# A Hyena long convolution: two of its three index exchanges go by DMA through DRAM instead of TensorE transposes, and the turn is ordered in phases

## The reference

```
hy = dwconv1d(hy_in, p['hy_conv_w'], p['hy_conv_b'])
v, x1, x2 = split(hy, 3)                         # 512 channels each, 2048 latent + 128 context tokens
k_f = hyena_filter_fft(L, ...)                   # rfft, length 2L, of an MLP's taps times a decay
z = x1 * fft_long_conv(v, k_f[:, 0], bias[0])
z = x2 * fft_long_conv(z, k_f[:, 1], bias[1])    # the second order needs the first one's z
# fft_long_conv(u, k_f, b) = irfft(rfft(u, n=2L) * k_f)[:L] + u * b
```

## Time and profile before

| | |
|---|---|
| median of 3 runs | 3146.26 us (3144.06 to 3146.97) |
| profiled execution, own time | 3143.5 us |
| its span | 3141.7 us |
| mean granted TensorE clock | 0.97 of full speed |
| busy, share of span | TensorE 94%, weight loads 81%, DVE 54%, ACT 30%, POOL 21% |
| `hyena` within the span | about 639 us to 1265 us |
| DMA | 252.84 MB, 80 GB/s over the span |

### The profile page before, as it was taken

The page is one execution under the profiler, slowest core; times in us unless marked ns, Lnnn a source line. Parts: engine busy times, 40 slices in busy tenths (PEclk is TensorE's granted clock), DMA queues, the critical chain, the costliest instruction groups (busy, mean ns, idle before and its releaser), DMA issues. The chain is left out here.

```text
span 3141.7 us, 40466 instructions
## 1 busy us (share of the span) xinstructions
PE 2947.5 (94%) x16404; PEld 2547.7 (81%) x16404; DVE 1689.8 (54%) x1888; ACT 928.5 (30%) x1608; POOL 668.8 (21%) x344
## 2 busy tenths in 40 slices
PE   5999999979999998598899999999999999999998
PEld 3777887878888888577788888888888887788886
DVE  6664564556666666464575565565565563322223
ACT  5443434145545554355510100100100103211111
POOL 3133233102222221344132222222222210000000
PEclk7999999989999999799999999999999999999999
DMA  6111221422121211444411111111111105322222
GB/s 228 69 58 70 73 79 63 123 118 86 56 86 61 82 59 53 135 134 154 154 35 55 48 34 55 48 34 55 48 34 55 48 25 190 119 75 75 82 86 72
DMA packets 92739, 252.84 MB, mean 80 GB/s; under 512 B 14846, under 2 KB 53246, under 8 KB 83198
## 3 DMA queue, kind: packets, MB, share of 16 engines
q1 hardware_dynamic: 92608, 251.00, 23.5%
HBM read 175.01 MB, written 75.96 MB: 80 GB/s over the span
## 5 line engine op out<-in xcount | busy, mean ns | idle before, releaser
L1813 PE MATMUL out_up_banks<-xh_rest,up_w_hi 128*128 128x512 f32 (+2 forms) x1408 | 493.6, 351 | 9.4 <-DVE xl_rest L1923 7.3
L1813 PE MATMUL out_up_banks<-xh_rest,up_w_lo 128*128 128x512 f32 (+2 forms) x1408 | 493.7, 351 | 0.0
L1813 PE MATMUL out_up_banks<-xl_rest,up_w_hi 128*128 128x512 f32 (+2 forms) x1408 | 493.4, 350 | 0.0
L1969 DVE SCALAR_TENSOR_TENSOR ffn_hidden<-grid,params,ffn_hidden 128x2048 f32<-128x2048 f32 x176 | 457.7, 2601 | 24.6 <-DVE ffn_hidden L1966 0.2
L2125 PE MATMUL down_banks<-down_hi,down_h_hi 128*128 128x512 f32 x748 | 293.4, 392 | 11.3 <-DVE down_gate L2206 5.3
L1813 PEld LDWEIGHTS out_up_banks<-xh_rest,up_w_hi 128*128 128x128 f32 x1408 | 266.5, 189 | 40.9 <-DVE xl_rest L1923 8.1
L2125 PE MATMUL down_banks<-down_lo,down_h_hi 128*128 128x512 f32 x748 | 292.6, 391 | 0.0
L2125 PE MATMUL down_banks<-down_hi,down_h_lo 128*128 128x512 f32 x748 | 292.5, 391 | 0.0
L1813 PEld LDWEIGHTS out_up_banks<-xl_rest,up_w_hi 128*128 128x128 f32 x1408 | 266.3, 189 | 30.7
L136 POOL TENSOR_TENSOR up_w_hi<-up_w_whole,zero 128x1024 fp32r<-128x1024 f32 x44 | 124.2, 2822 | 779.9 <-PE out_up_banks L1813 763.3
L1813 PEld LDWEIGHTS out_up_banks<-xh_rest,up_w_lo 128*128 128x128 f32 x1408 | 266.3, 189 | 28.3
(11 more groups left out here) (267 smaller groups left out, 5773.3 us busy)
## 6 DMA issues: line engine op xcount, KB each, us to landing
hidden_ff_dram<-ffn_hidden SPq DMA_DIRECT2D x22, 1088.0 KB, 4.8
up_w_whole<-w_up_in SPq DMA_DIRECT2D x44, 512.0 KB, 5.2
pre_dram<-in_result SPq DMA_DIRECT2D x16, 1088.0 KB, 4.0
down_h<-hidden_ff_dram SPq DMA_DIRECT2D x88, 192.0 KB, 2.3
wada_late<-w_ada_late_in SPq DMA_DIRECT2D x32, 512.0 KB, 3.7
down_x<-w_down_in SPq DMA_DIRECT2D x22, 512.0 KB, 3.7
in_w_whole<-w_in_in SPq DMA_DIRECT2D x20, 512.0 KB, 4.5
home<-x_rows_in SPq DMA_DIRECT2D x17, 512.0 KB, 6.7
```

The source lines that it names most:

```text
L1813: last = pe.matmul(out, weight[:, u, k], in_block(value, rest, b, k), start=(k == 0 and j == 0), stop=(k == KM - 1 and j == 2))
L1969: last = nc.vector.scalar_tensor_tensor(out=y, in0=window, scalar=weight, in1=y, op0=ALU.mult, op1=ALU.add)
```

## The change

The forward exchange of the convolution and the exchange of the filter leave TensorE. `first` becomes a single matmul per batch (table as weights, rows as 512 moving columns), whose result lies with frequency and slot in the partitions and channels in the free dimension. ACT copies it to one of four buffers `sent`; SP writes the 256 KB of a batch to a scratch tensor in DRAM and, once this has landed, reads them back in another order into `spectrum` (16 partitions of 32 pieces of 512 bytes). The read of batch j-2 stands in SP's queue behind the write of batch j. The filter does the same by `f_sent` and `f_spectrum`. The 64 transposes of `turn_back` and `f_turn_back` per turn and their 16 DVE copies are gone; `turn_pairs`, the back exchange, stays on TensorE.

The turn is ordered in phases: head (`turn_rows`, `first`), then a stretch of `taps`/`f_first` while the data are exchanged, then `second`/`back1`, then `turn_pairs`/`back2` with `f_second`. Gates and the stored z are moved at the turn's start, decay or v ahead of the back half, and ACT issues the modulation loads. `taps` and `swapped` now lie in the two halves of `rows`.

```diff
@@ the stages of a turn, and their order
-CONV_FORWARD = ([("turn_rows", j) for j in range(4)] + [("first", j) for j in range(8)]
-                + [("turn_back", j) for j in range(8)] + [("second", j) for j in range(8)])
-CONV_BACK = ([("back1", j) for j in range(8)] + [("turn_pairs", j) for j in range(8)]
-             + [("back2", j) for j in range(4)])
-
+def moved(stages, *names):
+
+    out = []
+    for stage, j in stages:
+        out.append((stage, j))
+        if stage in names:
+            out.append((stage + "_send", j))
+            if j >= 2:
+                out.append((stage + "_fetch", j - 2))
+            if j == 7:
+                out += [(stage + "_fetch", 6), (stage + "_fetch", 7)]
+    return out
...
+CONV_FIRST = (numbered("turn_rows", 0, 1) + numbered("first", 0, 1) + numbered("turn_rows", 2) + numbered("first", 2, 3)
+              + numbered("turn_rows", 3) + numbered("first", 4, 5, 6, 7))
+CONV_MIDDLE = (numbered("second", 0, 1, 2, 3) + [x for j in range(4) for x in (("back1", j), ("second", j + 4))]
+               + numbered("back1", 4, 5, 6, 7))
+CONV_LAST = (numbered("turn_pairs", 0, 1, 2, 3) + numbered("back2", 0) + numbered("turn_pairs", 4, 5) + numbered("back2", 1)
+             + numbered("turn_pairs", 6, 7) + numbered("back2", 2, 3))
+FILTER_FIRST, FILTER_SECOND = one_ahead("taps", "f_first"), numbered("f_second", *range(8))
+CONV_CHAIN = CONV_FIRST + CONV_MIDDLE + CONV_LAST
+FILTER_CHAIN = FILTER_FIRST + FILTER_SECOND
...
-ONLY_FILTER = FILTER_FIRST[:8] + CTX_TAPS + FILTER_FIRST[8:] + FILTER_SECOND + CTX_FILTER
-ONLY_CONV = interleave(CONV_FORWARD, CTX_FORWARD) + interleave(CONV_BACK, ADA + CTX_BACK)
...
-BOTH = (merge("ccfcccffccfccfccfcfccfccfccfcfccfccfccfcfccf", CONV_FORWARD, FILTER_FIRST,
-              [CTX_FORWARD[0], CTX_TAPS[0], CTX_FORWARD[1]])
-        + merge("ccfcfcfcfccfcfccffccccffcccffccffcff", CONV_BACK, FILTER_SECOND, ADA + [CTX_BACK[0], CTX_FILTER[0]]))
...
+MOVED = ("first", "f_first")
+IN_GAP = 13
+CTX_FORWARD = [("ctx_turn", 0), ("ctx_taps", 0), ("ctx_forward", 0)]
+SEND_FIRST = moved([("bulk_first", 0)] + CONV_FIRST, *MOVED)
+FILTER_ONCE = moved(interleave(FILTER_FIRST, [("ctx_taps", 0), ("load_v", 0)]) + [("load_second", 0)], *MOVED)
+WITH_FILTER = (CONV_MIDDLE[:2] + FILTER_FIRST[IN_GAP:IN_GAP + 1] + CONV_MIDDLE[2:3] + FILTER_FIRST[IN_GAP + 1:IN_GAP + 2]
+               + CONV_MIDDLE[3:4] + FILTER_FIRST[IN_GAP + 2:] + interleave(CONV_MIDDLE[4:], ada(1) + ada(2)))
+BOTH = moved(interleave(FILTER_FIRST[:IN_GAP], CTX_FORWARD + ada(0)) + WITH_FILTER + [("bulk_last", 0)] + interleave(CONV_LAST, FILTER_SECOND[:6], ada(3) + [("ctx_back", 0)])
+             + interleave(FILTER_SECOND[6:], [("ctx_filter", 0)]), *MOVED)
+ONLY_CONV = moved([("ctx_turn", 0), ("ctx_forward", 0)] + ada(0) + ada(1) + CONV_MIDDLE + ada(2)
+                  + interleave(CONV_LAST, ada(3) + [("ctx_back", 0)]), *MOVED)
+
+
+SLOT_ROWS = [j % 2 * 4 + j // 2 for j in range(8)]
+
+
+def across(rows):
+
+    return rows.rearrange("(k s) i c -> (s i) k c", s=4)
@@ hyena: buffers
+        sent = sb("hy_sent", [P, 4, 4, P])
+        spectrum = sb("hy_spectrum", [P, 32, P])
         spectrum_c = sb("hy_by_channel", [P, 64, 64])
-        spectrum_p = sb("hy_by_slot", [P, 32, P])
-        swapped = sb("hy_swapped", [P, 2, 4, P])
-        gated = swapped[:].rearrange("p j q c -> p j (q c)")
-        taps = sb("taps", [P, 2, 4, P])
-        f_by_channel = sb("f_by_channel", [P, 64, 64])
-        f_by_slot = sb("f_by_slot", [P, 2, 4, P])
+        swapped = rows[:, 8:].rearrange("p (j q) c -> p j q c", q=4)
+        gated = swapped.rearrange("p j q c -> p j (q c)")
+        taps = rows[:, :8].rearrange("p (j q) c -> p j q c", q=4)
+        f_sent = sb("f_sent", [P, 4, 4, P])
+        f_spectrum = sb("f_spectrum", [P, 32, P])
@@ hyena: each_turn
-            for stage, j in ONLY_FILTER:
+            for stage, j in FILTER_ONCE:
                 batch(stage, j, 0, 0, None, 0)
-            for ct in range(CT - 1):
-                for order in range(2):
-                    for stage, j in BOTH:
-                        batch(stage, j, ct, order, ct * 2 + order, ct * 2 + (order + 1))
-            for order in range(2):
-                for stage, j in (BOTH, ONLY_CONV)[order]:
-                    batch(stage, j, CT - 1, order, 2 * (CT - 1) + order, 2 * (CT - 1) + order + 1)
+            for stage, j in SEND_FIRST + [("load_tables", 0)]:
+                batch(stage, j, 0, 0, 0, 1)
+            for stage, j in FILTER_SECOND + [("ctx_filter", 0)]:
+                batch(stage, j, 0, 0, None, 0)
+            for turn in range(2 * CT):
+                ct, order = divmod(turn, 2)
+                for stage, j in (SEND_FIRST if turn else []) + (BOTH if turn < 2 * CT - 1 else ONLY_CONV):
@@ hyena: sync (the loading loop and load_ada of before are gone)
+                    if stage == "first_send":
+                        sp.wait_ge(out["first"], turn * 8 + j + 1)
+                        sp.dma_start(d["swap_first"][j], sent[:, j % 4]).then_inc(sent_done[j % 4], 16)
+                    elif stage == "f_first_send":
+                        sp.wait_ge(out["f_first"], f_turn * 8 + j + 1)
+                        sp.dma_start(d["swap_f_first"][j], f_sent[:, j % 4]).then_inc(f_sent_done[j % 4], 16)
+                    elif stage == "first_fetch":
+                        sp.wait_ge(sent_done[j % 4], sends_before("first", j, turn, f_turn) * 16 + 16)
+                        sp.dma_start(spectrum[SLOT_ROWS[j]:P:8], across(d["swap_first"][j])).then_inc(spectrum_loaded, 16)
+                    elif stage == "f_first_fetch":
+                        sp.wait_ge(f_sent_done[j % 4], sends_before("f_first", j, turn, f_turn) * 16 + 16)
+                        sp.dma_start(f_spectrum[SLOT_ROWS[j]:P:8],
+                                     across(d["swap_f_first"][j])).then_inc(f_spectrum_loaded, 16)
...
+                    elif stage == "bulk_first" and turn:
+                        wait_for_turn(turn - 1)
+                        if order == 0:
+                            store_z(ct - 1)
+                        load_gates(ct, order)
+                    elif stage == "bulk_last" and ct + 1 < CT:
+                        if order == 1:
+                            load_v(ct + 1)
+                        else:
+                            sp.wait_ge(out["taps"], ct * 16 + 16)
+                            sp.wait_ge(out["ctx_taps"], ct * 2 + 2)
+                            load_filter_inputs(ct + 1)
@@ hyena: tensor
                         if j == 0:
-                            pe.wait_ge(second_loaded, 32)
-                        for q in range(2):
-                            last = pe.matmul(bank[:, 256 * q:256 * q + 256], rows[:, 2 * j + q], first_t[:],
-                                             start=True, stop=True)
-                    elif stage == "turn_back":
+                            pe.wait_ge(first_loaded, 16)
+                        last = pe.matmul(bank, first_t[:, j % 2], rows[:, j // 2 * 4:j // 2 * 4 + 4]
+                                         .rearrange("p s c -> p (s c)"), start=True, stop=True)
+                    elif stage == "second":
                         if j == 0:
-                            pe.wait_ge(out["first"], turn * 8 + 8)
+                            pe.wait_ge(spectrum_loaded, turn * 128 + 128)
                         for q in range(4):
                             g = 4 * j + q
-                            last = pe.transpose(four(bank)[:, q], spectrum_c[:, 2 * g:2 * g + 2, :]
-                                                .rearrange("p r b -> p (r b)"), ident[:])
-                    elif stage == "second":
-                        pe.wait_ge(out["turn_back"], turn * 8 + j + 1)
+                            last = pe.matmul(four(bank)[:, q], second_t[:, g], spectrum[:, g], start=True, stop=True)
...
+                        last = pe.matmul(bank, f_first_t[:], taps[:, j % 2].rearrange("p q c -> p (q c)"),
+                                         start=True, stop=True)
+                    elif stage == "f_second":
+                        if j == 0:
+                            pe.wait_ge(f_spectrum_loaded, f_turn * 128 + 128)
@@ hyena: scalar
-                            last = nc.scalar.activation(spectrum_c[:, :, 8 * j + 4 * q:8 * j + 4 * q + 4],
-                                                        bank[:, 256 * q:256 * q + 256].rearrange("p (r b) -> p r b", b=4),
-                                                        ACT.Copy)
-                        last.then_inc(out[stage], 1)
+                        if sends_before(stage, j, turn, f_turn):
+                            act.wait_ge(sent_done[j % 4], sends_before(stage, j, turn, f_turn) * 16)
+                        nc.scalar.activation(sent[:, j % 4].rearrange("p q c -> p (q c)"), bank,
+                                             ACT.Copy).then_inc(out[stage], 1)
...
```

(12 more changed lines are left out.)

179 lines of the change are left out of this document (78 added, 101 removed).

## The result

The changed kernel takes 3129.65 us (median of 18 runs, 3120.18 to 3141.35), the kernel before 3145.39 us (18 runs beside them, 3140.26 to 3147.73): ratio 0.9955, 95% interval 0.9945 to 0.9965, or 15.7 us faster. Forecast were 47 us. The sign was right, the size three times too large. The runs of the changed kernel also scatter over 21 us, those of before over 7.5.

What follows compares the result with a forecast made beforehand. TensorE bounds hyena, 76.0 us a turn. Seven turns at 70.4 us save 39, the start 5, turn 7 3: 47 us off the profiled 3143.5 gives 3096.5, as median 3099 us; own range 3080 to 3113, overall 3060 to 3148.

Steps and rivals of the forecast that it cites:

- the start: From the first taps through turn 0's head: 5 us gained, between 0 and 8.
- turn 7: Last turn: 52 instead of 56.5 us, about 8 us of exchange open; with slow clock 3 us gained, between -3 and 6.
- the forecast's own signs of being wrong: Second waiting for DMA in every turn, granted clock below 0.9 on a turn's mean, or the old 4 us stall remaining.
- the rival of the lost interleaving: Middle and back half wait 5 us a turn more than put: 3134 us, up to 3150; chance 0.15.
- Middle: Phase of second and back1: 18.4 us of issue, product chain sets the pace, 21 us, plus 0.7 before turn_pairs.
- Clock: Slow clock after waits of 2 us in a turn: none to 3 us, 1.0 taken.
- the removed stall: TensorE's 4.03 us wait for taps before f_first, and 3.0 us lost to slow clock behind it: both go.
- x: DMA engine time of one 256 KB read back in 512-byte pieces: between 0.6 and 1.7 us, 1.2 taken.
- 8.7 + 8x: Length of the index exchange's writes and reads in one queue: 18.3 us for x = 1.2.
- the window: From the first write, 4.3 us into the head, until second needs everything at 25.0: 20.7 us; exchange inside by 2.4.
- reads are the bound: Second waits for the transposing reads; at x = 3 a 12 us wait, turn 85, about 3220 us; slower case's chance 0.11.
- The rival of the 19-fold read: Rearranged DMA read as transpose: 11 us a read, kernel some 600 us slower; size given no weight, direction some.

Runs made afterwards that it cites:

- o_ctx: Kernel before the change, with only the context stages ctx_taps and ctx_forward moved among the early first batches, no exchange by DMA: 3121.92 us.
- r_port: Changed kernel with both exchanges read back into 16 neighbouring partitions instead of 16 that are eight apart (output wrong): 3240.09 us.
- s_act: Changed kernel with v loaded first on SP, and the second table and two small ctx tables issued from ACT's queue: 3120.17 us.
- t7_noada: Changed kernel with turn 7's modulation loads cut from 512 KB to an eighth (output wrong): 3134.75 us.
- t7_order: Changed kernel with turn 7's first two modulation tiles moved from the gap to among second and back1: 3139.48 us.
- r_flat: Changed kernel with both exchanges read back in whole 16 KB rows instead of 32 pieces of 512 bytes (output wrong): 3127.47 us.

## Why the prediction was wrong in size

Two steps failed: the start, which was counted as a gain without the waits for its loads, and turn 7, whose sum left out 4.6 us of its own formula and whose exchange left out the modulation loads. The turns and the price of a read came out nearly as put. Of the forecast's own signs of being wrong only one came, the granted clock, and only in turn 7 (0.87 on the mean): they watch the turns, and the start has none. The measured time lies near that of the rival of the lost interleaving (3134 us), but not by its mechanism: middle and back half took 2.4 us a turn more than put, where that rival has 5.

**The turns held.** Forecast 70.4 us, measured 71.1; six of them gave 30.0 us where 33.6 were forecast. Head: `first` waits 1.66 us, put at 1.8. Head and gap together 24.2 us to `second`, put at 25.0; the 1.3 us of wait put in the gap are not there. Middle 24.2 on the mean, put at 21.7: this step was too low, by the wait of `f_first` 7 (1.7 put, 2.1 to 3.9 measured) and the slow clock. Back half and tail 22.7, put at 22.8; the wait there is 2.2 us, not 3.0. Clock: 23.9 us at the lower level in six turns, 2.0 us lost a turn, 1.0 put. What the forecast did not see is where the middle's surplus comes from. The wait of 1.7 us is 2.06 by DVE's order alone, with an addition of 1.67 us in it that was priced at 0.69. On top, in four of six turns, f_sent has four buffers, their writes queue behind everything on SP, and ACT, standing for one, holds the product chain. It also gave the removed stall 7.0 us (4.0 and 3.0 of clock); o_ctx shows 3.4, since the next limit on the same batch stood 2.1 us behind.

**The exchange's price held.** x was 1.2 us, by bounds of 0.6 and 1.7; the transfer records give 1.04. Turn 7 without the modulation loads' traffic: 20.5 less the 1.8 us from `first` to the first write is 18.7, and 8.7 + 8x gave 18.3. It fitted the window in 24 of 36 turns; in the other 12 the gates and, in 11 of them, z stood ahead, which the forecast had as nearly through by then. The rival "reads are the bound" was priced right as well: at a wait of 12 us a turn of 85 and 3220 us; r_port, with a wait of 10.7 us in turns 1 to 6, has turns of 85.8 and takes 3240. In part that is luck: the filter's reads are dearer there as well, and TensorE waits 3.7 us a turn for them, which the rival didn't count. The rival of the 19-fold read, a rule of the Trainium skill (DMA: Bandwidth & Descriptors, "Rules for kernel authors"), is not borne out: the 512-byte pieces cost 0.25 to 0.45 us a read of the exchange, 0.1 us of the DMA engines.

**Start: the step that failed most.** The forecast gained 5 us on the way to turn 0 and 5.6 in turn 0; measured is 6.5 lost up to turn 1, 17.1 us apart. It put 5 us for writes that queue behind the second table's 2 MB, and named no wait for v or of `ctx_filter`. In the trace 21.3 us are waits: for v behind the filter's exchange 6.2, the table 1.7, copies behind the exchange, itself behind the table, 5.9, and `ctx_filter` for a semaphore that counts the 2 MB `back1` table 7.5. s_act, which changes nothing but this, gives 13.2 back; of the wait for copies 4.4 us stay there, so most of it is not the table's.

**Turn 7: a sum that didn't follow its own formula, and loads not counted.** Forecast 53.5 us with its clock, measured 63.8. By the forecast's own formula `second` starts at 4.3 + 18.3 = 22.6 us into the turn; the sum put 10.5 + 7.5 = 18.0, having let the 4 us of context and modulation in the gap cover part of the wait and then not counted them as time. That is 4.6 us. `second` really started at 27.9: the other 5.3 are above all the two modulation loads (3.1 to 4.7 by t7_noada), which the prediction had "beside the chain", looking at ACT's issue and not at the bytes. The rest, 0.4, is not resolved.

**The sum:** 3.6 us in six turns, 17.1 in the start, 10.3 in turn 7, 1.9 from the later start of `hyena`: 32.9 between forecast and measured at its end, less the 4.6 that later blocks gave. That is the 28.4 us between the 3096.5 forecast for the profiled execution and its 3124.87. The medians are 30.7 apart (3099 and 3129.65); most of the rest is that the profiled execution of the changed kernel was a fast one. Not foreseen at all is the run-to-run scatter. Kernels with the same order of turns had 23.9 to 37.5 us at the lower clock in turns 1 to 6 and turn means of 71.1 to 73.2 us; late exchanges account for part, the cause of t7_order's high end stays open.

## What to carry to other kernels

When an exchange moves from an engine to DMA, go through every transfer that shares the queue or the engines with it in each phase, the first and the last round above all, and ask what each semaphore counts: of the 30.0 us that turns 1 to 6 gained here, start and turn 7 took 13.8 back. Before replacing work, move what stalls next to it: two reordered context stages gave more (23 us) than the replacement did (15.7). Where behind one wait the next stands ready, an edit that removes one shows little (3.9 and 7.3 us here); try them together (21.9 us) before giving either up.

## What the hardware showed that was not expected

- A read of 256 KB into 16 partitions costs 1.2 to 1.4 us more of exchange time each when they are neighbours instead of eight apart (r_port: 35.0 us for eight against 23.6 to 25.2), 2.16 us of the DMA engines against 1.04; piece size, 512 bytes or 16 KB, is worth 0.25 to 0.45 us of exchange time (r_flat: 21.6), 0.1 us of the engines.
- In the changed kernel a 256 KB write of the index exchange lands in 2.0 us at best, in turns 1 to 6, with the DMA engines 0.63 busy, in 4.0 at the median (5.3 at most), a read in 3.3, 4.2 and 5.3; over the whole run up to 8.8 and 9.2. The filter's, beside the bulk transfers, go up to 6.5 and 7.1 in the same turns. Put were 2.4 for a write and 2.5 to 3.5 for a read.
- Waits of 1.4 us already (`back2`, 1096.8 in the changed kernel's trace) were followed by a stretch of 3.4 us at 1.2 GHz in some turns and not in others of the same kernel; each costs a turn 1.6 us (70.1 against 68.5).
- The first addition of DVE in a turn with filter takes 1.67 us, the same operation elsewhere in the turn 0.69 (changed kernel, turns 0 to 6); POOL's products run beside it. No run tests the cause.
